# Four RMS norms: scaled halves and a transpose in place of a product with a diagonal

## The reference

```python
def rmsnorm(x, g):
    xf = x.astype(jnp.float32)
    y = xf * lax.rsqrt(jnp.mean(xf * xf, axis=-1, keepdims=True) + EPS)
    return (y * g.astype(jnp.float32)).astype(x.dtype)
...
    for l in range(DEPTH):
        h = rmsnorm(x, norm1_g[l])
        x = x + gated_parallel_mixer(h, ...)
        h = rmsnorm(x, norm2_g[l])
        x = x + conv_ffn(h, ...)
    return rmsnorm(x, final_g)
```

## Time and profile before

| | |
|---|---|
| median of 3 runs | 1582.04 us (1578.86 to 1585.06) |
| profiled execution, its own time | 1584.29 us |
| its span in the profile | 1582.5 us |
| PE busy | 1555.4 us, 98% |
| DVE busy | 1085.2 us, 69% |
| ACT busy | 931.1 us, 59% |
| granted TensorE clock, mean | 0.999 |

### The profile page before, as it was taken

How to read it: one execution, slowest core, us unless ns; L and a number is a source line. 1 busy time by engine, 2 the same in 40 slices (tenths; PEclk the granted TensorE clock), 3 DMA queues, 4 the chain that set the end, 5 groups by cost and what they waited for, 6 DMA issues and landing times.

```text
span 1582.5 us, 29407 instructions
## 1 busy us (share of the span) xinstructions
PE 1555.4 (98%) x12262; PEld 1425.9 (90%) x12262; DVE 1085.2 (69%) x1706; ACT 931.1 (59%) x1507; POOL 289.4 (18%) x210
## 2 busy tenths in 40 slices
PE   9999999999999999999999999899999999999998
PEld 7999998999899999999988998679988899889986
DVE  5775666887457765668864597689744688789644
ACT  6787756665457777566654665354433666664431
POOL 0000210443000002104420322019400021118200
PEclk9999999999999999999999999999999999999999
DMA  8344454565552434635554631245655535355651
GB/s 331 124 151 143 147 201 186 190 239 198 194 186 90 174 125 157 226 133 214 202 185 173 242 121 57 81 155 185 216 191 186 215 107 190 121 189 194 217 202 60
DMA packets 42324, 272.82 MB, mean 172 GB/s; under 512 B 4816, under 2 KB 4944, under 8 KB 13392
## 3 DMA queue, kind: packets, MB, share of 16 engines
q1 hardware_dynamic: 41184, 265.18, 46.8%
q10 hardware_dynamic: 1008, 5.77, 1.0%
HBM read 269.88 MB, written 1.05 MB: 171 GB/s over the span
## 4 chain that ended last, share of the span: by engine, by line
PE 89%; DVE 5%; ACT 4%; DMA 1%; issue 1%; SPq 0%; DVEq 0%; ACTq 0%
PE b_ps L403 16%; PE b_ps L406 16%; PE b_ps L405 16%; PE b_ps L463 10%; PE b_ps L464 10%; PE b_ps L466 10%; DVE b_wlo L330 1%; PE b_ps L1052 1%; PE b_ps L989 1%; DMA b_wraw<-in_w 1%; ACT b_S L962 1%; PE b_ps L1182 1%; PE b_ps L604 1%; ACT b_zrot L790 1%; PE b_ps L2568 1%
## 5 line engine op out<-in xcount | busy, mean ns | idle before, releaser
L330 DVE TENSOR_TENSOR b_wlo<-b_wraw,b_whi 128x2048 fp32r<-128x2048 f32 (+3 forms) x261 | 562.6, 2159 | 178.9 <-PE b_ps L466 126.7
L403 PE MATMUL b_ps<-b_H,b_whi 128*128 128x256 f32 x2152 | 605.1, 281 | 0.5 <-DVE b_trot L799 0.5
L406 PE MATMUL b_ps<-b_H,b_wlo 128*128 128x256 f32 x2152 | 598.5, 278 | 0.0
L405 PE MATMUL b_ps<-b_H,b_whi 128*128 128x256 f32 x2152 | 598.4, 278 | 0.0
L322 ACT ACTIVATE b_whi<-b_wraw 128x2048 fp32r<-128x2048 f32 (+3 forms) x262 | 466.6, 1782 | 207.6 <-PE b_ps L466 149.1
L403 PEld LDWEIGHTS b_ps<-b_H,b_whi 128*128 128x128 f32 x2152 | 404.9, 188 | 9.0 <-issue 6.8
L405 PEld LDWEIGHTS b_ps<-b_H,b_whi 128*128 128x128 f32 x2152 | 405.3, 188 | 0.7
L406 PEld LDWEIGHTS b_ps<-b_H,b_wlo 128*128 128x128 f32 x2152 | 405.4, 188 | 0.0
L1599 POOL TENSOR_TENSOR b_fl<-b_ab,b_fh 128x256 fp32r<-128x256 f32 x44 | 93.8, 2132 | 205.6 <-ACT b_fh L1572 205.6
L1520 POOL TENSOR_TENSOR b_mg<-b_mg,b_scr 128x256 f32<-128x256 f32 x32 | 31.5, 984 | 405.0 <-DVE b_scr L1505 405.0
L463 PE MATMUL b_ps<-b_whi,b_gh 128*128 128x512 f32 x256 | 99.7, 389 | 0.0
(11 more groups left out here) (361 smaller groups left out, 2447.9 us busy)
## 6 DMA issues: line engine op xcount, KB each, us to landing
b_wraw<-in_w SPq DMA_DIRECT2D x221, 1024.0 KB, 4.8
b_wraw<-in_w SPq DMA_DIRECT2D x35, 512.0 KB, 3.4
b_wraw<-in_w SPq DMA_DIRECT2D x6, 768.0 KB, 6.4
b_bias<-in_rpb SPq DMA_DIRECT2D x8, 512.0 KB, 6.1
b_gains<-in_gains ACTq DMA_DIRECT2D x4, 1024.0 KB, 4.9
b_X<-in_x ACTq DMA_DIRECT2D x2, 512.0 KB, 5.3
b_cA<-in_cA SPq DMA_DIRECT2D x2, 512.0 KB, 6.0
out<-b_X SPq DMA_DIRECT2D x4, 256.0 KB, 2.2
```

Of the source, the lines that this page charges most:

```text
L330: e.tensor_tensor(wlo[u % NLO][:, 0:n], raw[u % NRAW][:, 0:n], hi.bitcast(F32), ALU.subtract).then_inc(up("w_lo", "wlo", u))
L403: e.matmul(out, wh, x.hi[:, kk, :], start=k == 0, stop=False)
L405: e.matmul(out, wh, x.lo[:, kk, :], start=False, stop=False)
L406: ins = e.matmul(out, wl, x.hi[:, kk, :], start=False, stop=last)
```

## The change

At `n20`, `n11`, `n21` and `nf`, the diagonal is not built. Instead VectorE multiplies the first half of X (512 columns) by the inverse root into a tile `xs[0]`, and ScalarE the second half into `xs[1]`; X itself stays as it is. TensorE transposes the pieces of these two tiles against the identity. One pair of tiles serves both blocks of tokens, so the scaling of tb 1 waits until TensorE has turned the matching pieces of tb 0. The tiles are ones that lie idle then: two of the mixer's `S` tiles, or the feed-forward part's `rows`. At `n10` the product with the diagonal stays (the kind is now called `first`).

```diff
-    def first_rows_pe(e, w, job, key, kind):
+    def first_rows_pe(e, w, job, key, kind, xs=None):
...
-                turn_x_pe(e, w, key, kind, 1)
+                turn_x_pe(e, w, key, kind, 1, xs)
...
+    def rms_scale_dve(e, w, key, tb, xs):
+        s = tst[:, tb, :]
+        w.wait_ge(*at(key, "root", tb))
+        e.reciprocal(s[:, 4:5], s[:, 3:4]).then_inc(up("x_rinv", key, "rinv", tb))
+        w.wait_ge(*at(key, "rinv", tb))
+        if tb:
+            w.wait_ge(*at("full", ("xt", key, 0, 1)))
+        e.tensor_scalar(xs[0], x_half(0, tb), s[:, 4:5], None, ALU.mult).then_inc(up("x_n", key, "xn", 0, tb))
+
+    def rms_scale_act(e, w, key, tb, xs):
+        w.wait_ge(*at(key, "rinv", tb))
+        if tb:
+            w.wait_ge(*at("full", ("xt", key, 0, 3)))
+        e.activation(xs[1], x_half(1, tb), ACT.Copy, scale=tst[:, tb, 4:5]).then_inc(up("x_n_act", key, "xn", 1, tb))
...
-                if kind == "rms":
+                if kind == "first":
                     w.wait_ge(*at(key, "diag", tb))
                     ins = e.matmul(out, x, diag[:, tb, :], start=True, stop=True)
                 else:
                     w.wait_ge(*at(key, "xn", f // 4, tb))
-                    ins = e.transpose(out, x, ident)
+                    ins = e.transpose(out, x if xs is None else xs[f // 4][:, f % 4 * P:f % 4 * P + P], ident)
...
             if kind == "rms":
                 rms_sum_act(e, w, key, j, tb, ("free", (job.key, j, tb)))
+                if j == 1:
+                    rms_scale_act(e, w, key, tb, xs)
...
                 if kind == "rms":
-                    rms_diag_dve(e, w, key, tb)
+                    rms_scale_dve(e, w, key, tb, xs)
...
+                self.scaled = [S_ring[0][:, :], S_ring[1][:, :]]
...
+                self.scaled = [self.rows[:, 0, :], self.rows[:, 1, :]]
```

More of the change, by code:

```diff
@@ L592, in ln_scale_act, with turn_x_pe @@
         e.activation(x_half(1, tb), x_half(1, tb), ACT.Identity, bias=s[:, 5:6], scale=s[:, 4:5]).then_inc(up("x_n_act", key, "xn", 1, tb))
-    def turn_x_pe(e, w, key, kind, tb):
+    def turn_x_pe(e, w, key, kind, tb, xs=None):
         for q in range(4):
@@ L724, in single, with end_pe @@
         return job.nk <= job.kpart
-    def end_pe(e, w, job, key, kind):
+    def end_pe(e, w, job, key, kind, xs=None):
         blocks = row_blocks(job)
@@ L733, in end_pe, with end_act @@
         if kind != "last":
-            turn_x_pe(e, w, key, kind, 0)
+            turn_x_pe(e, w, key, kind, 0, xs)
         row_pe(e, w, job, *blocks[-1], q)
-    def end_act(e, w, job, key, kind, gkey=None, bkey=None):
+    def end_act(e, w, job, key, kind, gkey=None, bkey=None, xs=None):
         last = last_unit(job)
@@ L750, in end_act, with end_dve @@
                 h_act(e, w, key, gkey, bkey, tb)
-    def end_dve(e, w, job, key, kind, gkey, bkey, scale, need=None):
+    def end_dve(e, w, job, key, kind, gkey, bkey, scale, need=None, xs=None):
         last = last_unit(job)
@@ L1317, in pe @@
             banks.assign(lin=EVERY, att=EVERY)
-            first_rows_pe(e, w, self.v, f"n1{self.l}", "rms")
+            first_rows_pe(e, w, self.v, f"n1{self.l}", "rms", ffns[self.l - 1].scaled if self.l else None)
             for j in range(4):
@@ L1361, in pe @@
                 tile_pe(e, w, self.gates[br] if what == "gate" else self.brs[br], j)
-            end_pe(e, w, self.out, f"n2{self.l}", "rms")
+            end_pe(e, w, self.out, f"n2{self.l}", "rms", self.scaled)
         def act(self, e, w):
@@ L1411, in act @@
                 self.branch_act(e, w, what, *i)
-            end_act(e, w, self.out, f"n2{l}", "rms", f"norm2_g{l}")
+            end_act(e, w, self.out, f"n2{l}", "rms", f"norm2_g{l}", xs=self.scaled)
         def bias_sp(self, e, w, rq):
@@ L1489, in dve @@
                 self.branch_dve(e, w, what, *i)
-            end_dve(e, w, self.out, f"n2{l}", "rms", f"norm2_g{l}", None, 1.0)
+            end_dve(e, w, self.out, f"n2{l}", "rms", f"norm2_g{l}", None, 1.0, xs=self.scaled)
         def branch_dve(self, e, w, what, br, j):
@@ L1543, in pe @@
             banks.assign(lin=EVERY, att=EVERY)
-            first_rows_pe(e, w, self.first, f"n2{self.l}", "rms")
+            first_rows_pe(e, w, self.first, f"n2{self.l}", "rms", mixers[self.l].scaled)
             for m in self.order:
@@ L1550, in pe @@
                         tile_pe(e, w, self.up_, 2 * m + g)
-            end_pe(e, w, self.down, self.next[0], "rms")
+            end_pe(e, w, self.down, self.next[0], "rms", self.scaled)
         def act(self, e, w):
@@ L1572, in act @@
                     e.activation(self.f.hi[:, m, :], A[:, 0, :], ACT.Copy).then_inc(up("f_hi", k, "hi", m))
-            end_act(e, w, self.down, self.next[0], "rms", self.next[1])
+            end_act(e, w, self.down, self.next[0], "rms", self.next[1], xs=self.scaled)
         def dve(self, e, w):
@@ L1593, in dve @@
                     e.tensor_tensor(A[:, 0, :], A[:, 0, :], A[:, 1, :], ALU.mult).then_inc(up("gated", "gated", l, m))
-            end_dve(e, w, self.down, self.next[0], "rms", self.next[1], None, 1.0)
+            end_dve(e, w, self.down, self.next[0], "rms", self.next[1], None, 1.0, xs=self.scaled)
         def pool(self, e, w):
@@ L2217, in pe @@
             banks.assign(lin=ALL, att=ALL)
-            first_rows_pe(e, w, self.v, "nf", "rms")
+            first_rows_pe(e, w, self.v, "nf", "rms", ffns[1].scaled)
             for what, i in self.steps[:7]:
@@ L2714, in tensor_program @@
         for tb in range(2):
-            turn_x_pe(e, w, "n10", "rms", tb)
+            turn_x_pe(e, w, "n10", "first", tb)
         for l in range(2):
```

## The result

The changed kernel takes 1586.9 us (median of 20 runs, 1579.5 to 1592.72), the kernel before 1582.9 us beside it (20 runs, 1578.78 to 1587.24). The ratio is 1.0023, interval 1.0012 to 1.0034: slightly slower, where 1.94 us faster was forecast, and above the range. It is within the 0.5% that was given 0.92. In a later set of runs the same kernel gave 1.0008 (0.9998 to 1.0018). So the puzzle is this: at the four norms the change does what was worked out and somewhat more, and yet the whole is not shorter.

A forecast was written before the change was run, and what follows sets the result against it. TensorE, busy 98% of the span and 89% of the chain, was taken as the bound. Savings of 1.38 us (tb 0) and 0.56 us (tb 1) sum to 1.94, so 1582.04 - 1.94 = 1580.1 us; range 1576.5 to 1583.8.

The forecast's parts named there:

- Turn of tb 0 on TensorE: At all four norms, eight transposes take 0.82 us instead of 1.70; TensorE is 0.73 early at n20, 0.71 at n11.
- The half on VectorE: At each turn, VectorE's scaling of half of X takes 0.54 us, replacing the diagonal's 0.29.
- The weights' second part: Behind tb 0's turn, L330 comes no sooner; TensorE keeps 0.72 at n20 and n21, loses 0.03 at n11 and nf.
- The idle of 0.15 ahead of the turn: Sign at n20: an idle of about 0.15 us before tb 0's first transpose, named to VectorE's half.
- Turn of tb 1: At all four norms, first transpose to first L466 takes 2.11 us, today 2.25; TensorE keeps 0.14 each, 0.56 in all.
- The sum at the norms: Over the four norms, 1.38 us from tb 0 plus 0.56 from tb 1 gives 1.94 us saved.
- TensorE's busy time: Sign over the whole kernel: TensorE's busy time falls by about 7 us, its idle time grows by about 5.
- Moved or added elsewhere: Outside the norms, no transfer, bank or queue moves; all work behind arrives earlier as a whole, at no cost.
- the 6.2 us between the shown runs: Whole kernel: scatter of the runs shown, 6.2 us, taken as three times the effect.
- Rival 1: At the norms, TensorE keeps everything: 6.4 us less, 1575.6 us; chance 0.08.
- Rival 2: Behind the norms, a stage paced by VectorE, ScalarE or weights' transfers leaves 0 to 0.6 us gain, 1581.8; chance 0.17.
- Rival 4: Behind each of eight turns, 4 us at the lower clock cost 2 us, 16 in all: 1598 us; chance 0.02.

The follow-up runs named there:

- the small matmul: One short float32 matmul, result overwritten, added behind the eight transposes of each feed-forward part; changed kernel with 128 columns: 1577.81 us, ratio 0.9978.
- after: The changed kernel as first measured and profiled: median 1586.9 us, ratio 1.0023; its profiled execution 1583.55 us.
- before: The kernel before the change, with the diagonal at all four norms: median 1582.9 us beside the first result.
- its halves: Changed kernel with transposes for tb 0 alone (1583.6 us, 1.0027) or tb 1 alone (1586.92 us, 1.0047), the other block keeping its diagonal.
- the late transposes: The feed-forward part's eight transposes moved from behind its first 48 matmuls to ahead of its last 144; kernel before with this: 1582.19 us, 0.9997.
- e10: Changed kernel with each feed-forward part's eight transposes moved from behind its first 48 matmuls to ahead of its last 144: 1588.36 us, ratio 1.0033.
- e1: The changed kernel run again unchanged: 1580.55 us, ratio 1.0008 to the kernel before.
- e6: Changed kernel with two more long-passed waits in TensorE's queue at each of the four norms: 1583.75 us, ratio 1.0034.
- e7: Changed kernel with one more long-passed wait in TensorE's queue at each of the four norms: 1584.99 us, ratio 1.0030.
- e0: The kernel before run again unchanged, for the scatter between executions: 1578.69 us, ratio 0.9994.
- e4: Kernel before with one more long-passed wait in TensorE's queue ahead of the turn of tb 1 at n20: 1579.14 us, ratio 1.0004.

## Why the prediction was wrong, step by step

- **Turn of tb 0 on TensorE, 0.82:** measured 0.82. The half on VectorE is 0.49, not 0.54: the row taken had one more scalar. ScalarE's 0.72 lies between the bounds 0.63 and 0.81 and is hidden, as said.
- **The weights' second part:** the first bank's reader starts 0.44 behind the first transpose, not 0.50. The idle of 0.15 ahead of the turn, named as a sign, isn't in the profile: TensorE's last step into the turn is 0.32, 0.09 longer than a normal one. With 0.05 less on VectorE that lets L330 begin 4.74 behind the inverse root's start (253.06 - 248.32) instead of 4.85 (254.41 - 249.56, rows 4, 5), where no change was forecast; an earlier L330 was one of the named signs of being wrong, and at n11 too it comes 4.55 behind VectorE's scale (437.65 - 433.10) instead of 4.63 (439.97 - 435.34, rows 6). The limits were named rightly: n11 waits 1.05 (forecast about 1.1). With tb 0's transposes alone the four norms give 1.84 us; forecast 1.38.
- **Turn of tb 1:** from the first transpose to the first L466 of tb 1 it is 260.25 - 258.32 = 1.93, forecast 2.11. The waits appear where they were put, for the high part 0.24 (load 0.48) and then for the low (load 0.35), but shorter than the 0.6 and 0.25. Alone it gives 0.97; forecast 0.56.
- **The sum at the norms:** 2.7 us; forecast 1.94. Mechanism right, somewhat too small.
- **TensorE's busy time:** 3.7 us less, forecast about 7. Eight turns of 1.95 became 1.06, 7.1 less, and this execution's clock falls stretched other matmuls by 3.4. Idle grew by 2.9, forecast about 5. The two waits behind tb 1 are shorter, and 1.5 of what idle was added is the wait at 904, which the forecast doesn't have.
- **Moved or added elsewhere, the step that failed:** "Behind the norms, every engine's work is ordered by the same semaphores, and arrives earlier as a whole." The work does arrive earlier and in the same order, but it doesn't take the same time: the stretches behind the norms run at 113 or 118 ns per matmul, and which it is goes with a few nanoseconds in the steps ahead of them. The changed kernel meets the slow pace more often; a feed-forward part alone is worth 4.1 us, more than the whole gain. And arriving early, TensorE waits longer in four of its five profiles without the small matmul. In the sum of the prediction both stood at nothing; measured, on average over the profiles, they are 3.3 and 1.9 us against 2.4 gained. A second place of the prediction hid this: it took the 6.2 us between the shown runs as scatter that would fall on both kernels alike. Over the 20 profiles it is largely these paces, and their odds were not the same for the two kernels.
- **Rival 1** (TensorE keeps everything) falls by n11's wait. **Rival 2** (given back later) has the right place. Its mechanism, a later stage paced by another engine, is the smaller part: the wait of 1.5 us for ScalarE at 904 in after's profile. The larger part is TensorE's own matmuls, and together they can take more than was gained, which its price of 0 to 0.6 us left did not allow. **Rival 4** (the clock falls behind the turns) falls: the granted clock is 1.00 in the 20 us around each of the four norms in after's profile, as here around n20 (the fall at 905.8 is farther off, behind a wait of 1.50):

```profile
248.00:268.00 20.00, 19.76 (x105) 16.23 (x104) 13.37 (x24) 15.07 (x27) 0.00 (x0) 1.00 0.28 94
```

The Trainium skill, "TensorE: Matmul & The Clock Gate", Part 4: PE-mode transpose, whose rule was weighed for it, says that transposes don't count as PE-busy in the way matmuls do; for runs of eight between matmuls, no run here shows a fall from it.

**Open.** What resource makes the two paces, and why the row products carry a phase into them. Why the changed kernel meets the bad phase more often: the odds were seen (of the feed-forward stretches before and its variants have 12 of 12 fast, the changed kernel and its halves, without the small matmul or the late transposes, 4 of 14), not derived. Why the second part of e10 met the slow pace. What TensorE waits for at the "issue" waits between 970 and 1010, and why e1, e6, e7 and e10 wait longer there than both halves. The reading of steps of 226 and 116 ns is a correlation; the small matmul shows that the pace can be set at the switch, not how. 128 columns was the third size tried, and where another size or place would do better was not tried.

## What to carry to other kernels

When a change is worth less than the scatter, measure its place by itself in the trace, and then compare the long stretches that it does not touch: count the matmuls per window at granted clock 1.00. Then add up TensorE's waits behind the changed places: work that arrives early may only wait. If the same matmuls run at two paces, a median judges in part the luck of the phase and not the change; fix the pace first (here by one short matmul at the switch, an estimate of some 0.2 us, as eight take 1.70, against the 4.1 us that a slow stretch costs) and judge then. And a 98% busy TensorE is not at its peak: 30 matmuls in 90 us were missing with no idle time at all.

## What the runs showed of the hardware

- Back-to-back pairs of load and matmul of 128x256 have two steady paces, 113.3 and 117.8 ns (4%), at the same granted clock, kept through up to 912 matmuls until the next interruption. Between executions of one program the choice can differ (the MLPs of before and e0). Between programs the odds seem to: the feed-forward stretches of before and its variants were fast in 12 of 12, those of the changed kernel and its halves in 4 of 14.
- One float32 matmul of 128 columns ahead of such a stretch left it fast in 10 cases of 10; with 64 or 96 columns it was slow in 3 of 6.
- A run of eight float32 transposes takes 0.82 us on TensorE where eight float32 matmuls of 128 columns take 1.70: about half; the trace has 8 records for the one and 16 for the other.
- A wait that has long been passed needn't show as an instruction of its own (391 semaphore instructions with and without it in e4), a second one does (403 against 399 for four norms in e6).
- The granted clock fell to the lower level for some 3.4 us at a time, none to two times in a profile before TensorE's work ended, each worth 1.7 us. Two of these falls, in after and e1, came 1.5 and 0.9 us behind the end of a wait of 1.5 us.
